# Layer 2's attention entry: one PSUM read pulled forward, the rope-key split moved to GpSimd, values in other banks, banks awaited where they are used

## The reference

```python
def mixer_a(...):   # layer 1: windowed attention, 16 query heads, 4 key heads, with a sink, rope on q and k
def mixer_b(h, hc, w_in, q_norm_g, w_uq, kv_norm_g, w_ukv, w_o, cos, sin, ctx_out):   # layer 2
    cq, ckv, kr, g = jnp.split(h @ w_in, splits, axis=-1)
    q = (rmsnorm(cq, q_norm_g) @ w_uq).reshape(bsz, S, B_HEADS, B_NOPE + B_ROPE)
    qn, qr = q[..., :B_NOPE], apply_rope(q[..., B_NOPE:], cos, sin)
    kv = (rmsnorm(ckv, kv_norm_g) @ w_ukv).reshape(bsz, S, B_HEADS, B_NOPE + B_V)
    kn, v = kv[..., :B_NOPE], kv[..., B_NOPE:]
    kr = apply_rope(kr, cos, sin)
...
    s = (einsum(qn_b, kn_all) + einsum(qr_b, kr_all)) * scale
    p = jax.nn.softmax(s, axis=-1)
    return einsum(p, v_all)
...
def second_block(...):   # third layer: neighbourhood attention for 8 heads, then an mLSTM for 4 heads
```

## Time and profile before

| what | value |
|---|---|
| three runs | 1254.59, 1255.1, 1256.2 us |
| the profiled execution's own time | 1257.04 us |
| its span (first to last instruction) | 1255.0 us |
| mean granted TensorE clock over the span | 0.964 of full speed |
| TensorE busy | 1151.3 us (92%) |
| VectorE, ScalarE, GpSimd busy | 807.3, 649.1, 348.8 us |

### The profile page before, as it was taken

The page is one execution under the profiler, slowest core; times in us unless marked ns, Lnnn a source line. Parts: engine busy times, 40 slices in busy tenths (PEclk is TensorE's granted clock), DMA queues, the critical chain, the costliest instruction groups (busy, mean ns, idle before and its releaser), DMA issues.

```text
span 1255.0 us, 19725 instructions
## 1 busy us (share of the span) xinstructions
PE 1151.3 (92%) x7368; PEld 922.1 (73%) x7368; DVE 807.3 (64%) x1581; ACT 649.1 (52%) x1316; POOL 348.8 (28%) x192
## 2 busy tenths in 40 slices
PE   4799999999998899998999999999899978999786
PEld 0487787877886688876787787987777756767565
DVE  5365666676668336445787786468655583887865
ACT  4512555555557337533776677465655443453623
POOL 0532111111110316552000013055312135443631
PEclk9799999999998899998999999999999997999899
DMA  9451343422102211232202210431123015124102
GB/s 342 170 200 51 102 168 138 149 93 102 29 24 102 86 50 52 85 118 49 63 27 85 77 34 11 153 97 52 48 71 126 17 30 173 26 76 150 52 1 67
DMA packets 35146, 111.17 MB, mean 89 GB/s; under 512 B 4500, under 2 KB 7060, under 8 KB 34668
## 3 DMA queue, kind: packets, MB, share of 16 engines
q1 hardware_dynamic: 35052, 109.92, 26.6%
HBM read 103.23 MB, written 2.15 MB: 84 GB/s over the span
## 4 chain that ended last, share of the span: by engine, by line
PE 67%; DVE 17%; ACT 6%; DMA 4%; issue 4%; POOL 2%; SPq 0%; POOLq 0%; DVEq 0%; ACTq 0%
PE PS L626 27%; PE PS L609 14%; PE PS L743 7%; PE PS L731 7%; DMA AF<-wstream 4%; PE PS L971 3%; PE PS L661 2%; DVE AF L2214 2%; DVE AD L2153 2%; PE PS L914 2%; PE PS L820 1%; PE PS L957 1%; PE PS L642 1%; ACT AF L1181 1%; POOL AR L2290 1%
## 5 line engine op out<-in xcount | busy, mean ns | idle before, releaser
L626 PE MATMUL PS<-AR 128*128 128x512 f32 (+1 forms) x2304 | 483.0, 367 | 16.1 <-POOL AR L2290 7.4
L626 PEld LDWEIGHTS PS<-AR 128*128 128x128 f32 x2304 | 389.0, 193 | 90.3 <-issue 20.9
L2290 POOL TENSOR_TENSOR AR<-AF,AR 128x1024 fp32r<-128x1024 f32 x99 | 243.0, 2462 | 696.7 <-ACT AR L1059 696.7
L609 PE MATMUL PS<-AR 128*128 128x256 f32 (+4 forms) x1284 | 252.4, 335 | 20.6 <-POOL AR L2367 5.6
L609 PEld LDWEIGHTS PS<-AR 128*128 128x128 f32 (+1 forms) x1284 | 185.5, 195 | 59.3 <-issue 26.4
L1190 ACT ACTIVATE AF<-PS 128x512 f32<-128x512 f32 (+3 forms) x192 | 124.5, 649 | 118.8 <-PE PS L731 115.0
L1181 ACT ACTIVATE AF<-PS,AF 128x512 f32<-128x512 f32 (+3 forms) x192 | 140.9, 734 | 23.9 <-DVE AF L2132 12.6
L731 PE MATMUL PS<-AF 128*128 128x128 f32 x864 | 128.8, 277 | 9.8 <-DVE AF L1825 5.4
L731 PEld LDWEIGHTS PS<-AF 128*128 128x128 f32 x864 | 101.3, 141 | 34.5 <-issue 15.6
L743 PE MATMUL PS<-AF 128*64 128x128 f32 x1728 | 117.7, 282 | 5.0 <-DVE AF L1832 4.8
L1059 ACT ACTIVATE AR<-AF 128x1024 fp32r<-128x1024 f32 x99 | 103.0, 1050 | 28.3 <-DMA AF<-wstream 16.2
(11 more groups left out here) (192 smaller groups left out, 1231.0 us busy)
## 6 DMA issues: line engine op xcount, KB each, us to landing
AF<-wstream SPq DMA_DIRECT2D x171, 512.0 KB, 5.2
AD<-rows SPq DMA_DIRECT2D x4, 1024.0 KB, 9.7
AF<-x_in SPq DMA_DIRECT2D x2, 1024.0 KB, 8.9
out<-AF SPq DMA_DIRECT2D x16, 128.0 KB, 1.9
AF<-AF SPq DMA_DIRECT2D x28, 64.0 KB, 2.0
AF<-rpb_band SPq DMA_DIRECT2D x8, 224.0 KB, 4.7
BIAS<-rpb_band SPq DMA_DIRECT2D x8, 224.0 KB, 4.6
AF<-ctx_in SPq DMA_DIRECT2D x1, 1024.0 KB, 5.8
```

Of the source, the lines that this page charges most:

```text
L609: mm = pe.matmul(out, stationary, moving, start=i == 0, stop=i == len(products) - 1)
L626: mm = pe.matmul(out[:, 0:t1 - t0], a, b, start=k == 0 and i == 0, stop=k == nk - 1 and i == 2)
L2290: pool.tensor_tensor(w[:, 1, :], RAW[:, c % N_RAW, :], w[:, 0, :].bitcast(F32), ALU.subtract).then_inc(lo_done, 1)
```

## The change

1. `rope_turned` can be told that its first half was already done. The PSUM read of the last turn, `B.qr3.rot`, is issued by VectorE at once after the gate of `B.g7`, its sum stays behind `low_b`.
2. VectorE no longer splits the roped keys. GpSimd does it, after its last `cosine`: it waits for the read of `B.kr.1`, for the key's rope sum, for `B.g7.x`, and for its own earlier work, then casts, waits for the cast, and subtracts.
3. The second half of the values stands in banks 4, 5, 6, 7, 2, 3 instead of 7, 0, 1, 2, 3, 7. They no longer take part in the ring, so every later `spread` result is one bank earlier in the ring than it was.
4. `attend` waits for banks 0 and 1 ahead of the first scores, for 2 and 3 ahead of the second, and for 4, 5, 6 ahead of the first turn. This holds for all three attentions.

```diff
@@ task_plan
-    for t in range(T // P):
-        spread(f"B.v.{t}.1", "B.uv")
+    for t, b in enumerate((4, 5, 6, 7, 2, 3)):
+        task(f"B.v.{t}.1", b, "B.uv")
@@ attend on TensorE
-                for b in (0, 1, 2, 3, 4, 5, 6, 7):
-                    last = max((tasks[n][1] for n in opened if tasks[n][0] == b), default=0)
-                    if last:
-                        pe.wait_ge(acc_read[b], last)
+                before = list(opened)
+
+                def banks_read(first, *banks):
+                    for b in banks if first else ():
+                        last = max((tasks[n][1] for n in before if tasks[n][0] == b), default=0)
+                        if last:
+                            pe.wait_ge(acc_read[b], last)
+
...
+                        banks_read(m == m0, 0, 1)
                         scores(2 * m)
                     if m0 <= m - behind < m1:
+                        banks_read(m - behind == m0, 4, 5, 6)
                         turn(2 * (m - behind))
...
+                        banks_read(m == m0, 2, 3)
                         scores(2 * m + 1)
@@ VectorE
-            def rope_turned(name, tmp, dst):
+            def rope_read(name, tmp):
+                read(dve.tensor_tensor(tmp, wait_acc(name), ROPE[:, 1, :], ALU.mult), name)
+
+            def rope_turned(name, tmp, dst, taken=False):
...
-                read(dve.tensor_tensor(tmp, wait_acc(name), ROPE[:, 1, :], ALU.mult), name)
+                if not taken:
+                    rope_read(name, tmp)
...
-            wait_read("B.kr.1")
-            split(KB[64:96, 0, 0, 0, :], KB[64:96, 1, 0, 0, :], KRF[64:96, :], kr_split, 1)
+            rope_read("B.qr3.rot", QR[:, 3, :])
...
-            rope_turned("B.qr3.rot", QR[:, 3, :], QR[:, 3, :])
+            rope_turned("B.qr3.rot", QR[:, 3, :], QR[:, 3, :], taken=True)
@@ GpSimd, between cosine and the low parts of the roped queries
+            wait_read("B.kr.1")
+            pool.wait_ge(rope_sum, 11)
+            b, i = tasks["B.g7.x"]
+            pool.wait_ge(acc_ready[b], i)
+            pool.wait_ge(cos_done, ropes[0])
+            pool.wait_ge(lo_done, fed[0])
+            pool.tensor_copy(KB[64:96, 0, 0, 0, :], KRF[64:96, :]).then_inc(kr_high, 1)
+            pool.wait_ge(kr_high, 1)
+            pool.tensor_tensor(KB[64:96, 1, 0, 0, :], KRF[64:96, :], KB[64:96, 0, 0, 0, :].bitcast(F32),
+                               ALU.subtract).then_inc(kr_split, 1)
+            pool.wait_ge(kr_split, 1)
```

More of the change, by code:

```diff
@@ L448, in build @@
         pt_ready, pt_read, pv_done, o_read = (sem(n) for n in ("probs_turned", "turned_read", "pv_done", "o_read"))
+        kr_high = sem("rope_keys_high")
         kr_split, kr_in, qb_in = sem("rope_keys_split"), [sem("rope_keys_in0"), sem("rope_keys_in1")], [
```

## The result

The changed kernel took 1241.98, 1242.89, 1242.97 and 1304.42 us, median 1242.93 us; the fourth ran in a slow state (mean granted clock 0.838, the others 0.972 to 0.977) and is left out of every comparison. The kernel before took 1254.24 to 1256.2 us beside it, median 1254.84. The ratio is 0.991, 95% interval 0.9891 to 0.9929: the changed kernel is 11.9 us, about 0.9%, faster. The profiled span fell from 1255.0 to 1241.2 us, by 13.8.

What follows compares the result with a forecast made beforehand. TensorE was taken to bound the kernel (67% of the chain), with idle time at the attention entries. Layer 2's 6.0 us plus layer 1's 2.4 made 8.4, so 1255.1 - 8.4 = 1246.7 us, range 1244.8 to 1250.3.

Steps and rivals of the forecast that it cites:

- Layer 2: Layer 2's entry: 7.0 us gained at the first maximum less 1.0 us lost, 6.0 us in sum (4.6 to 7.3).
- First maximum: Layer 2's entry: first maximum of scores at 585.1 instead of 592.12, VectorE being free at 584.8; 7.0 us earlier.
- The price for GpSimd's pass: Layer 2's first scaling of probabilities, held by GpSimd's low part of weights `B.uq1`: about 1.0 us lost.
- cast: GpSimd's cast of layer 2's keys, ahead of its subtract: taken as 1.3 us, between bounds of 0.73 and 1.83.
- first scores: Layer 2's entry: they wait next for the query transfers, taken as there at 583.7 (583.3 to 584.1).
- The rule of the Trainium skill: Layer 2's first scaling: VectorE scaling and GpSimd operation exclude each other for the whole instruction; cost 1.0 to 1.2 us.
- The other rule of the Trainium skill: GpSimd's first cast: first call about 6 us, giving 1252.7; expensive cast's chance 0.04 for a few us, 0.03 more.
- Layer 1: Layer 1's entry: first scores run under the gates, clock stays high, third scores at 116.6 instead of 119.04; 2.4 us.
- Layer 3 and the ring: Layer 3's first scores still wait for bank 1, and ring banks are reused at distance five as before: 0.
- stretches of low clock that fall otherwise: Range allowance for the whole kernel: 0.6 us at the low end, one microsecond at the high end.
- A: Theory in the experiments: entries give what was forecast; the rest is which stretches of low clock an execution meets.
- B: Theory in the experiments: forecast missed a lasting term of about 4 us further on, in ring, queues or later waits.

Runs made afterwards that it cites:

- e4: Changed kernel with ScalarE's high part and GpSimd's low part of weights `B.uq1` made earlier, the low part behind the first `QRL`; 1245.78 us.
- e10: Changed kernel with layer 2's rope key split back on VectorE; 1246.88 us, ratio 0.9937.
- e16: Changed kernel with one added VectorE maximum (0.7 us) ahead of layer 1's attention; 1246.64 us, ratio 0.9946.
- e13: The kernel before, unchanged, profiled again; span 1249.0 us.
- e14: The kernel before, unchanged, profiled a third time; span 1247.8 us.
- e3: Kernel before with only the banks of the second half of the values changed; 1247.8 us, ratio 0.9966.
- e12: Changed kernel with the first scores' waits in `attend` back in one place for all eight banks; 1245.57 us, ratio 0.993.
- e1: Changed kernel with the bank ring advanced by six, so results behind the values keep their earlier banks; 1242.53 us, ratio 0.9918.
- e9: Changed kernel, unchanged, timed again as the mark for undoing parts one by one; 1243.14 us, ratio 0.9918.
- e5: Changed kernel, unchanged, timed again beside versions with added delays; 1244.98 us, ratio 0.9948.
- e17: Changed kernel, unchanged, many executions; 1242.06 us, ratio 0.9918.
- e18: Changed kernel with the `B.uq1` weight split taken earlier, the kernel of e4 timed once more; 1247.17 us, ratio 0.9957.
- e6: Changed kernel with one added VectorE maximum (0.7 us) ahead of layer 2's first maximum; 1241.8 us, ratio 0.9925.
- e2: Kernel before with only the one-by-one bank waits in `attend`; 1250.16 us, ratio 0.9972.

## Why the prediction came out as it did

**Layer 2, 6.0 us forecast, 6.0 measured.** First maximum 7.0 us earlier forecast, 7.0 seen (the shift went from 0.5 at 535 us to 7.6 at the first exponential). The price for GpSimd's pass, 1.0 us, came as 1.56 instead of 0.62 us. The steps inside, with the 0.5 us by which this execution was ahead at 535 us taken off the forecast instants: cast 1.3 us forecast, 0.82 measured; keys at 577.5 forecast, 577.2 seen; first scores 583.2 forecast, 582.53 seen (the last query transfer landed at 582.44, and TensorE ended the values at 582.53, so the transfers cost it no time); first maximum 584.6 forecast, 584.56 seen. The instant was right by a different last wait: the forecast had the scores end it and VectorE free 0.3 us before; in the trace the scores came earlier and VectorE's copies, which end at 584.52, ended it. That the two lay so close together is luck. The forecast had no pause ahead of the second scores; TensorE idled 0.80 us there for the last copy. The rule of the Trainium skill ("SBUF — State Buffer", "Who interferes with whom") was right here: the trace has 1.56 us beside GpSimd, and e4 has 0.62 without. The forecast priced the scaling by it and the rope's sum beside `QRL` at 0.69 us, as if free; that held in the changed kernel and not in e10 and e16. The other rule of the Trainium skill ("GPSIMD Engine Reference", "Instruction dispatch", about 6 us for a first call) did not show: the program's first cast on GpSimd took 0.82 us, and it began 0.17 us behind ScalarE's read of the product that it waits for, so nothing of that size stood ahead of it either.

**Layer 1, 2.4 us forecast, 2.2 measured in the first pair, 0.7 against e13 and e14.** The step was priced as if before always ran its entry at the low clock. The profiled execution did, behind 2.05 us of idle time, and so did e3 and e12. e13 and e14 did not, behind 2.08 and 2.05 us, so 1.5 of the 2.2 us were the clock's, and the first pair gave 1.7 back between 335 and 423 us.

**Layer 3 and the ring, 0 forecast.** e1 bears it out for the ring. In layer 3 the pause ahead of the first scores is 0.98 us after and 0.93 before, so the change gives nothing there; what differs there are stretches of low clock.

**The step that failed is the allowance in "How the numbers follow": 0.6 us at the low end, and one microsecond at the high end, for "stretches of low clock that fall otherwise".** It measured 5.2 to 5.8 us in the first set: 11.9 less the 6.1 to 6.7 that the edited stretches give. Behind 770 us alone, executions of the changed kernel differ by 6.1 us (478.1 to 484.2) and of before by 3.8. Several places there cost up to 1.6 us each if the clock falls, and the first three, at 783, 902 and 934 us, have the same pauses in all 20 traces (1.86, 2.77 to 2.79 and 2.08 to 2.10 us), with a fall behind them in 7, 12 and 16 of the 20. From 75.8 to 770 us, where the change works, before's three executions take 693.0 to 694.0 us and the changed kernel's four 687.0 to 687.6: 6.1 us, with little scatter, or 6.7 by the two entries alone (0.7 and 6.0). The medians moved by 8 to 12 us in four sets.

What is over that goes with the clock. The mean granted clock is 0.967 over the 85 executions of before and 0.972 over the 26 of the changed kernel. A fit with one slope for both puts the changed kernel 5.7 us (plus or minus 1.0) under before at the same clock, with 6.1 us for each 0.01; of the 8.9 us between the means, 3.2 are then the clock's. This is an estimate, and it agrees with the 6.1 us of the edited stretches. It does not say which falls are fewer: of the changed kernel's four traces two (after, e9) have less low clock behind 770 us than any of before's three, and two (e5, e17) have more.

The local terms themselves came to 6.1 to 6.7 us against 8.4 forecast, so the forecast erred in both directions. That its 8.4 stood close to one set (e5, 7.9 us) is luck, and it was low against the others.

**A or B.** B's lasting term of about 4 us in ring, queues or later waits has e1, the spread of e5, the equal pauses, the steps at the falls and the 5.7 us at equal clock against it. A held for the place and kind of the surplus, but in its simple form, luck of single executions, it is not enough: e17's median gain of 10.2 and the loss of e4 and e18 in two sets point to the kernel. Which detail of a kernel's timing decides whether the clock falls behind a given pause stays open; that the edit causes it in any plannable way is not shown.

**Best version.** None measured beat the changed kernel with certainty. e6 had the lowest median (1241.8, four executions), with more work in it, which is a reason against reading anything into it.

## What to carry to other kernels

Price an edit by the stretch in which it works: the distance between two marks around layer 2's entry repeated within 0.5 us in before and 0.1 in the changed kernel, while whole executions of one program spread over 10. (Around layer 1's entry before repeated within 1.6 us only, the clock's share.) Before building on one profile, take a second of the same kernel: a pause followed by low clock in one had full clock in the next, and a term of 2.4 us turned into 0.7. Where a kernel has many pauses at which TensorE's clock may fall, the range needs the sum of those stakes, not one microsecond, and a local gain of under 1 us is to be judged by many executions or not at all. Where two engines' instructions hold each other, look at how far apart they start: here a start 0.35 us later made an entry of 13.4 us one of 15.5 (e16), the clock's fall behind it included.

## What the hardware showed that was not expected

- Equal pauses, unequal clock. Behind 1.86 us idle near 783 us the window's clock was 0.83 in the first of before and in e18, and 1.00 in the first of after and in e14. At layer 1's entry a pause of 2.05 us brought the low clock in the first of before, in e3 and in e12, and 2.05 and 2.08 us brought none in e14 and e13.
- The head of the kernel, which all versions share, took 73.0 to 75.9 us in the seven executions of the table.
- VectorE and GpSimd hold each other for more kinds of work than the scaling: the rope's sum of 128x512 took 1.73 and 1.76 instead of 0.69 us (e10, e16). The first profile of before had this already: at 549.00 and 556.71 the same sum took 2.43 us beside GpSimd's weight passes. A column of 128x1 with both operands in SBUF was held as well (timeline of the changed kernel's layer 1 entry, the held one and the next):

```profile
115.30 0.46 DVE L1835 TENSOR_TENSOR AF<-AF 128x1 f32<-128x1 f32 x1 [0.17 <-ACT AF L1189]
...
116.39 0.15 DVE L1835 TENSOR_TENSOR AF<-AF 128x1 f32<-128x1 f32 x1
```

- VectorE's cast of 32x768 took 1.50 us in e2 and e3, where GpSimd's `QRL` had begun 0.2 us ahead of it, and 0.78 in e10, where little of `QRL` was left; GpSimd's took 0.82, while its subtract of the same size took 1.84.
